# Output gates of two branches as sets of seven quarter products inside the recurrence, with a new order for VectorE and memory loaded in halves

## The reference

```python
def first_block(x, mem, ...):
    h = rms_norm(x, norm_g[l])
    p = h @ w_in[l]
    y_a = rwkv7_mix(...) * silu(z_a)                     # the recurrence
    y_b = sliding_window_sink_attn(...) * silu(z_b)
    y_c = memory_cross_attn(p_xq, mem, mem_norm_g, ...) * silu(z_c)
    gates = sigmoid(p_gate).reshape(bsz, t, 3, 1024)
    merged = (gates[:, :, 0] * (y_a @ w_proj_a) + gates[:, :, 1] * (y_b @ w_proj_b)
              + gates[:, :, 2] * (y_c @ w_proj_c))
    x = x + merged @ w_out

def hybrid_layer(x, mem, ...):                           # the second layer
    # top-k sparse attention (8 heads) beside a 31-tap causal convolution, w_out_2,
    # cross attention to a memory of 256 rows, a feed-forward net with a 3-tap convolution
return rmsnorm(x, norm_final_g)
```

## Time and profile before

| | |
|---|---|
| median of 3 runs | 1705.4 us (1705.25 to 1709.52) |
| the profiled execution's own time | 1704.97 us |
| its span | 1703.2 us |
| TensorE busy | 1610.0 us (95%) |
| VectorE busy | 1078.9 us (63%) |
| ScalarE busy | 384.4 us (23%) |
| GpSimd busy | 130.7 us (8%) |

### The profile page before, as it was taken

One profiled execution on the slowest core, in us unless ns is written; L12 is line 12 of the kernel. 1 busy time (PEld: TensorE's weight loads), 2 busy tenths in 40 slices (PEclk: granted clock), 3 DMA queues, 4 the chain that ended last, 5 costly groups with the idle time before them and its releaser, 6 DMA issues.

```text
span 1703.2 us, 23651 instructions
## 1 busy us (share of the span) xinstructions
PE 1610.0 (95%) x9170; PEld 1115.1 (65%) x9170; DVE 1078.9 (63%) x2127; ACT 384.4 (23%) x750; POOL 130.7 (8%) x121
## 2 busy tenths in 40 slices
PE   7989997899999999999999988999999999999997
PEld 6866543345555555675854456648785888888885
DVE  5976856852333333377848999566767787877453
ACT  3334344431111111131125433320301000000000
POOL 0020300031000000000007700000000000000000
PEclk9999998999999999999999998999999999999998
DMA  7212110111111111123212221122022222223331
GB/s 269 72 60 74 50 62 27 48 50 38 38 39 38 40 37 49 59 75 124 99 62 75 75 75 63 50 87 84 29 75 74 75 99 77 97 82 97 91 89 63
DMA packets 46271, 122.05 MB, mean 72 GB/s; under 512 B 5137, under 2 KB 19217, under 8 KB 45777
## 3 DMA queue, kind: packets, MB, share of 16 engines
q1 hardware_dynamic: 45072, 115.89, 20.0%
q10 hardware_dynamic: 864, 3.35, 0.5%
q0 software_dynamic: 224, 1.31, 0.2%
HBM read 118.43 MB, written 2.10 MB: 71 GB/s over the span
## 4 chain that ended last, share of the span: by engine, by line
PE 72%; DVE 23%; ACT 2%; issue 2%; DMA 1%; ACTq 0%; DVEq 0%
PE bank L608 17%; DVE arena L1796 5%; DVE arena L1787 4%; PE vpair L1264 4%; PE opair L1264 4%; PE bank L1264 3%; PE abank L1264 3%; PE opair L638 2%; PE vpair L638 2%; PE abank L1018 2%; PE vpair L1018 2%; PE opair L1293 2%; PE vpair L1293 2%; DVE tmp L1787 2%; PE abank L638 2%; DVE arena L2419 2%
## 5 line engine op out<-in xcount | busy, mean ns | idle before, releaser
L608 PE MATMUL bank<-h,ring 128*128 128x512 f32 x816 | 380.2, 606 | 1.1 <-ACTq L1401 1.1
L608 PEld LDWEIGHTS bank<-h,ring 128*128 128x128 f32 x816 | 149.0, 191 | 160.6 <-issue 152.9
L1787 DVE TENSOR_TENSOR arena<-arena,vpair 128x256 f32<-128x256 f32 x87 | 36.7, 421 | 190.3 <-PE vpair L1018 117.6
L608 PE MATMUL bank<-arena,ring 128*128 128x512 f32 (+1 forms) x320 | 122.2, 523 | 2.5 <-DVE arena L1787 2.3
L1787 DVE TENSOR_TENSOR arena<-ring 128x512 f32<-128x512 f32 (+2 forms) x132 | 78.4, 594 | 70.6 <-DMA ring<-weights 50.9
L1796 DVE SCALAR_TENSOR_TENSOR arena<-arena,cols 128x512 f32<-128x512 f32 (+1 forms) x133 | 98.2, 738 | 4.7
L608 PEld LDWEIGHTS bank<-arena,ring 128*128 128x128 f32 x320 | 59.3, 194 | 48.0 <-issue 40.2
L857 PE MATMUL vpair<-arena 128*128 128x256 f32 (+4 forms) x224 | 49.2, 451 | 29.0 <-DVE arena L1787 12.9
L1787 DVE TENSOR_TENSOR arena<-arena 128x256 f32<-128x256 f32 (+1 forms) x114 | 57.3, 503 | 6.0 <-PE bank L911 2.2
L857 PEld LDWEIGHTS vpair<-arena 64*128 64x128 f32 (+1 forms) x224 | 31.3, 207 | 45.0 <-DVE arena L1787 15.3
L2692 POOL TENSOR_TENSOR arena<-arena 128x512 f32<-128x512 f32 x43 | 55.9, 1299 | 16.6 <-ACT arena L1660 13.4
(11 more groups left out here) (359 smaller groups left out, 2985.3 us busy)
## 6 DMA issues: line engine op xcount, KB each, us to landing
ring<-weights SPq DMA_DIRECT2D x185, 512.0 KB, 3.6
ring<-weights SPq DMA_DIRECT2D x68, 128.0 KB, 2.3
x<-xt SPq DMA_DIRECT2D x8, 512.0 KB, 7.1
ring<-weights SPq DMA_DIRECT2D x40, 64.0 KB, 2.0
out<-h SPq DMA_DIRECT2D x8, 256.0 KB, 2.0
cst<-cst_in ACTq DMA_DIRECT2D x1, 1504.0 KB, 8.0
arena<-memt ACTq DMA_DIRECT2D x1, 1024.0 KB, 7.9
arena<-mem2t POOLq DMA_DIRECT2D x1, 1024.0 KB, 5.0
```

The source lines that it names most:

```text
L608: last = mm(o[:, 0:n], weight(), src, start=c == 0, stop=c == len(srcs) - 1)
L1787: do(V.tensor_tensor(out, a, b, op), sig)
```

## The change

1. **Gates of branches b and c by sets.** For each pair of tiles, one set of seven quarter products in four groups (2, 2, 2 and 1 quarters) goes through the two filling banks (`gate_set`), then two projections. An iteration has 7 + 2 + 2 = 11 quanta; the last fill is 2 and no longer 3. VectorE puts the quarters together in `gate_out` (`first_quarter` to `last_quarter`, 8 operations of 128x256 a set), ScalarE applies one tanh to both tiles, and `gated` multiplies. The four weight sums of the next set stand in `gated(n, 1)`, at the head of the next iteration; those of set 0 ahead of the loop, after a wait for `silu_done`. The weights' order in `source` follows, in more and smaller transfers.
2. **The memory in halves.** `mem[:, 0:4]` comes by ScalarE's queue as before, `mem[:, 4:8]` by SP's, ahead of all else there. Their readers wait for each half.
3. **VectorE's order at the front.** `apply_norm` stands ahead of the weight sums of set 0; the sums of sets 4 and 5 stand right behind takes 2 and 3, ahead of refinements.
4. **Paired scores.** VectorE takes the maxima of a pair of attention jobs in the first one's step (window and sparse attention).
5. **Gates of branch a.** TensorE no longer waits for `c_read` there; VectorE forms the weight sums earlier, and the squares of the second memory and the angles change places with takes.
6. **Constants.** Seven unused 128-column blocks are gone, so the transfer of 1504 KB is 1056 KB.

The diff, cut to its core:

```diff
--- before.py
+++ after.py
...
-for _name, _n in (("ones", P), ("head_ones", P), ("ident", P), ("ident64", HD), ("rot", P), ("dup0", P), ("dup1", P),
-                  ("rotdup0", P), ("rotdup1", P), ("rot2", P), ("rot2dup0", P), ("rot2dup1", P),
...
-        gt = [tmp[:, 3], thz[:, 1]]
...
+        gate_sums, gate_out = take(4, T), take(2, T)
...
+        QUARTERS = (("dve", 0), ("dve", 0), ("dve", 0), ("dve", 2 * KD))
+        stage("gates", *[*QUARTERS, V4, V4] * len(GATES))
+        GATE_SETS = len(GATES)
+        GATE_PAIRS = 7 + 2 + 2
...
-        GATED = stage_groups("gates", "gates a")
+        GATED = [("dve", 4), ("dve", 4), ("dve", 4), ("act", 2), ("dve", 4), ("dve", 4)] * GATE_SETS
...
-        source += [*range(YA, LWA), *range(V_ + 4 * KD, GLU)]
+        source += range(YA, LWA)
+        GATE0 = V_ + 4 * KD
+        for q in range(GATE0, GATE0 + 24 * len(GATES), 48):
+            for a, n in ((0, 8), (8, 4), (12, 8), (20, 4)):
+                source += [*range(q + a, q + a + n), *range(q + 24 + a, q + 24 + a + n)]
+        source += range(GATE0 + 24 * len(GATES), GLU)
...
-        GATE_PAIRS = 12
...
-                    if n or name == "gates a":
+                    if n and name == "front sets":
                         pe.wait_ge(c_read.sem, s)
                     product(d[:, 0:HT], summed(3), lambda k: h[:, 4 + k, HT:T])
...
+            def gate_set(n):
+
+                s = set_number("gates", n)
+                w = [weight() for _ in range(2 * KD)]
+                sums = set_sums("gates", n)
+
+                def product(o, lhs, rhs):
+                    for k in range(4):
+                        last = mm(o, lhs(k), rhs(k), start=k == 0, stop=k == 3)
+                    return last
+
+                def summed(i):
+                    pe.wait_ge(wsum_ready.sem, 4 * s + i + 1)
+                    return lambda k: sums[i][:, tok(k)]
+
+                o = dense_bank()
+                product(o[:, 0:HT], lambda k: w[k], lambda k: h[:, k, 0:HT])
+                yield
+                end_group(product(o[:, HT:T], lambda k: w[4 + k], lambda k: h[:, 4 + k, 0:HT]))
+                yield
+                o = dense_bank()
+                product(o[:, HT:T], summed(0), lambda k: t_h[0][:, k])
+                yield
+                end_group(product(o[:, 0:HT], summed(1), lambda k: t_h[1][:, k]))
+                yield
+                o = dense_bank()
+                product(o[:, 0:HT], summed(2), lambda k: t_h[2][:, k])
+                yield
+                end_group(product(o[:, HT:T], lambda k: w[12 + k], lambda k: t_h[3][:, k]))
+                yield
+                o = dense_bank()
+                end_group(product(o[:, 0:HT], summed(3), lambda k: h[:, 4 + k, HT:T]))
+                yield
+
+            def gate_stream(ybs, ycs):
+
+                for n in range(GATE_SETS):
+                    yield from gate_set(n)
+                    for _ in range(2):
+                        yield from dense_pairs((ybs, ycs)[n % 2])
...
-            work = stream([hs, ybs, hs, ycs] * len(GATES))
+            work = gate_stream(ybs, ycs)
...
-                    fill(work, 3)
+                    fill(work, 2)
...
             def gate():
 
-                o = dense_in()
                 n = st["gate"]
                 st["gate"] += 1
-                if n >= 2:
-                    act.wait_ge(gate_used.sem, n - 1)
-                do(fn(gt[n % 2], o[:, :], ACT.Tanh, scale=0.5), dense_act)
+                act.wait_ge(gate_summed.sem, n + 1)
+                do(fn(gate_out, gate_out, ACT.Tanh, scale=0.5), gate_th)
...
-            act.dma_start(mem, memt).then_inc(mem_in.sem, 16)
+            act.dma_start(mem[:, 0:4], memt[:, 0:4]).then_inc(mem_in.sem, 16)
...
+                act.wait_ge((mem_in if i < 4 else mem_late_in).sem, 16)
...
+                    for j in scored_in(i, n, first):
+                        scored(j)
...
-            dve.wait_ge(mem_in.sem, 16)
             for i in range(KD):
+                dve.wait_ge((mem_in if i < 4 else mem_late_in).sem, 16)
...
-                g = start[name] + n
-                if n >= 2:
+                g = start[name] + n * (6 if name == "gates" else 1)
+                if n >= 2 and name != "gates":
...
-            fast_weights("front sets", 0)
             for i in range(4):
                 dve.wait_ge(x_in[i].sem, 16)
             apply_norm("norm_g")
+            fast_weights("front sets", 0)
...
+            fast_weights("front sets", 3)
             for n in range(2):
-                fast_weights("front sets", 3 + n)
                 plain_take("front sets", 2 + n, yc[:, 2 * n:2 * n + 2, :])
+                fast_weights("front sets", 4 + n)
                 for i in range(2 * n, 2 * n + 2):
                     ri = rinv_refined(i)
                     stt(xq[:, i, :], xq[:, i, :], col("xq_g"), ri, MUL, MUL, norm_applied)
-            fast_weights("front sets", 5)
...
+            def first_quarter():
+
+                a, b = halves_of(dense_in())
+                copy(c21, a)
+                tt(c11, c21, b, ADD, dense_dve)
+
+            def second_quarter():
+
+                a, b = halves_of(dense_in())
+                tt(c21, c21, a, ADD)
+                tt(c12, c21, b, ADD, dense_dve)
+
+            def third_quarter():
+
+                a, b = halves_of(dense_in())
+                tt(c22, c12, a, ADD)
+                tt(c21, c21, a, ADD)
+                tt(c21, c21, b, ADD, dense_dve)
+
+            def last_quarter():
+
+                a, _ = halves_of(dense_in())
+                tt(c12, c12, a, ADD, dense_dve)
+                signal_now(gate_summed)
+
+            def gated(n, i):
+
+                if i and n + 1 < GATE_SETS:
+                    fast_weights("gates", n + 1)
+                dve.wait_ge(gate_th.sem, n + 1)
+                j = GATES[n // 2 * 2 + i]
+                o = dense_in()
+                stt(tmp[:, 2] if n % 2 else partial[j], gate_out[:, i, :], 1.0, o[:, :], ADD, MUL, dense_dve)
+                if n % 2:
+                    tt(partial[j], partial[j], tmp[:, 2], ADD)
+
+            reading = {"done": 0, "todo": [f for n in range(GATE_SETS) for f in (
+                first_quarter, second_quarter, third_quarter, last_quarter,
+                lambda n=n: gated(n, 0), lambda n=n: gated(n, 1))]}
+            dve.wait_ge(silu_done.sem, 12)
+            fast_weights("gates", 0)
...
+                if i == 2:
+                    fast_weights("gates a", 2)
                 ri = rinv_in(i)
                 stt(tmp[:, 0], rwy[:, i, :], col("lnx_g", i), ri, MUL, MUL)
                 stt(tmp[:, 0], tmp[:, 0], col("lnx_b", i), bonus[:, i, :], ADD, ADD)
                 tt(ya[:, i, :], tmp[:, 0], ya[:, i, :], MUL, norm_applied)
             bufs["lo"] = sq
-            fast_weights("gates a", 2)
             plain_take("gates a", 1, gates_a[:, 2:4, :])
+            fast_weights("gates a", 3)
+            angles(pos2_in, "freq2", trig_ready, 1, pos2_raw, ang)
+            plain_take("gates a", 2, gates_a[:, 4:6, :])
             for i in range(KD):
                 add_square(i, of=mem2_squares)
-            fast_weights("gates a", 3)
-            plain_take("gates a", 2, gates_a[:, 4:6, :])
-            angles(pos2_in, "freq2", trig_ready, 1, pos2_raw, ang)
...
+            sp.dma_start(mem[:, 4:8], memt[:, 4:8]).then_inc(mem_late_in.sem, 16)
```

93 lines of the change are left out of this document (36 added, 57 removed).

## The result

| | before | changed |
|---|---|---|
| median | 1707.22 us (1705.25 to 1709.52, 4 runs) | 1691.7 us (1690.65 to 1692.35, 4 runs) |
| span of the profiled execution | 1703.2 us | 1690.4 us |
| ratio | | 0.9914, interval 0.99 to 0.9929 |

Faster by 15.5 us in these runs. The four runs of before stand in two pairs, near 1705.3 and near 1709.3, so its median of 1707.22 lies between them. In three later sets of runs before had medians of 1705.2 to 1705.3, and in one of them the changed kernel 1690.25 (ratio 0.991, 0.9897 to 0.9924); the gain is 13.5 to 15.5 us, by the runs that are compared. The forecast was 1683.9, against 1704.97: 21 us were forecast, some 15 came.

A forecast was written before the change was run, and what follows sets the result against it. TensorE, nearly without gaps, was taken to bound the recurrence and VectorE the sparse attention. From 1704.97 us, -12.5 (recurrence), -1.9 (memory), -2.9 (`apply_norm`) and -3.8 (front sums) gave 1683.9 us, range 1673 to 1696.

The forecast's parts named there:

- one quantum less in eight iterations: Recurrence: each of eight iterations has 11 quanta for 12, some 1.7 us each, so 13.6 us go.
- weight sums of set 0 ahead of the first masks: First iteration of the recurrence: VectorE's sums after silu delay level 1, +1.1 us (bounds 0 and +3).
- VectorE's quarters in the levels, quarter-width quanta: Recurrence levels: 3.7 us of new operations a set hidden in VectorE's idle time, quanta of both kinds cost the same: 0.
- weight sums at the head of the iterations: Head of each iteration: four sums, 2.9 us, fit in slack of 1.5 to 1.8 us, larger with transposes: cost 0.
- memory in halves: Start: memory split over two queues, second product group near 16.7 for 18.55, -1.9 us (bounds 0 and -3.2).
- `apply_norm` first: Front set 0: put ahead of the weight sums, both TensorE waits go, -2.9 us (bounds 0 and -2.9).
- sums of sets 4 and 5: Front sets: four sums move into VectorE's idle time, its chain ends earlier, -3.8 us (bounds -1.0 and -3.8).
- Rival (b): Start: memory halves bring nothing, since bytes set the start; 1685.8 us, chance 0.13.
- Rival (a): Sparse attention: paired scores pay too, TensorE's seven waits (12.2 us) close; 1671.7 us, chance 0.12.
- (c): Front: its time is given back in a later wait, only the recurrence counts; 1692.5 us, chance 0.17.
- (d): Recurrence: the removed quantum was cover for a VectorE chain, a wait replaces it; 1697.5 us, chance 0.09.
- (e): Head of each iteration becomes the bound, slower; 1736.7 us if sums and quarters lie wholly bare, chance 0.04.

The follow-up runs named there:

- 5: The kernel before, every second gate tile of branches b and c made from six of its eight blocks, 11 full-width quanta an iteration: 1691.52 us, ratio 0.9923.
- 6: The changed kernel with the weight sums of set 0 behind the first iteration's masks instead of ahead: 1691.3 us, ratio 0.9918.
- 1: The kernel before with only the gates of branches b and c by sets and the smaller constants: 1696.41 us, ratio 0.9945.
- 9: The changed kernel with four more 128x512 sums on VectorE ahead of each of the seven in-loop sets of weight sums: 1698.95 us, ratio 0.9961.
- 3: The kernel before with the memory in halves alone: 1706.66 us, ratio 1.0001.
- 4: The changed kernel with the memory loaded whole on ScalarE's queue as before: 1691.3 us, ratio 0.9916.
- 2: The changed kernel without the gates by sets and without the smaller constants: 1701.46 us, ratio 0.998.
- 7: The changed kernel with both halves of the memory on SP's queue, ahead of the weights: 1691.57 us, ratio 0.9918.
- 11: The changed kernel with the weight sums of set 0 behind the first iteration's masks, run again: 1691.57 us, ratio 0.9915.
- 12: The changed kernel run once more, unaltered, in one call with the masks-first repeat: 1690.25 us, ratio 0.991.

## Why the prediction was right, and by how much its terms were off

| term | forecast | measured | from |
|---|---|---|---|
| one quantum less in eight iterations | -13.6 | -13.7 | 5 |
| weight sums of set 0 ahead of the first masks | +1.1 | +1.0 | 6 |
| VectorE's quarters in the levels, quarter-width quanta | 0 | +2.1 (+2.4 less the fifth iteration's wait) | 1, 5, 6 |
| weight sums at the head of the iterations | 0 | 0, cover 1.55 to 1.95 | 9 |
| memory in halves | -1.9 | 0 | 3, 4 |
| `apply_norm` first | -2.9 | -2.55 | 2 |
| sums of sets 4 and 5 | -3.8 | -3.8 | 2 |
| paired scores, gates of branch a | 0 | 0 | 2, table |

The measured time lies 7.8 us above the forecast, well inside the range, and the three largest terms (the gates, `apply_norm`, the sums of sets 4 and 5) came where they were forecast. With all of it the measured parts make -10.6 - 2.55 - 3.8 = -17.0 us, and the medians -13.5 to -15.5. The rest is in single product groups that run slower behind a wait in some profiles. One of them is in the last stretch, from the end of the sparse attention to the end: the same sixteen records took 8.83 us for 7.13 in nine of the thirteen new profiles, behind a wait of 2.0 us in all of them. The first row is before, the second changed:

```profile
1116.80 7.13 PE L1221 MATMUL vpair<-arena,ring 128*128 128x512 f32 x16 [1.99 <-DVE arena L1796]
```
```profile
1102.90 8.83 PE L1259 MATMUL vpair<-arena,ring 128*128 128x512 f32 x16 [2.00 <-DVE arena L1832]
```

Of the changed kernel and its variants (experiments 4, 6, 7, 9, 11 and 12) six profiles in seven have it, of the others three in seven. Whether the change makes it more frequent, or chance does, no run shows.

Two steps failed. The first is the sentence that the quarters in the levels "are hidden". They are shorter than VectorE's idle time there, which is what I looked at, but the next level's sum starts 0.07 us late behind them, at three places in an iteration. With the quarter-width quanta a little longer (1.99 for 1.98, or 1.93 for 1.91 to the next group), where the prediction had "quanta of both kinds cost the same", that makes 0.3 us an iteration. A count of idle time cannot show that; it needs the time from the product to the sum.

The second is the memory. I took the second group (18.55) as waiting for panels. It had no wait in its row: TensorE ran from 9.57 to 26 without a gap, so the start alone set it, and the start hung on the half on ScalarE's queue, which landed near 8.7 for 9.1. Rival (b) was right that this term is 0. The section "Issuing engines are not separate DMA queues" of the Trainium skill's page "DMA: Bandwidth & Descriptors" says that transfers run on the same 16 DMA engines and interleave, whichever engine issued them; the bytes moved from 2 to 9 us agree (2.61 before, 2.36 changed and 2.42 MB in experiment 7). The term was not 0 for want of an earlier start, though: in experiment 7 TensorE did start 0.8 us earlier and lost it to the third panel.

Two smaller errors cost little. The prediction had the slack at the head larger where transposes stand ahead of level 1, and experiment 9 found it smaller, 1.55 for 1.95 us. And it took both of TensorE's waits for `h` (2.9 us) as gained, where one of 0.58 for a weight sum came in and 2.55 us were left.

Rival (a) can be judged in the sparse attention. Seven waits of 12.2 us on the scores are gone, and in their place TensorE waits in more and shorter pieces:

```profile
PE abank L929 <- DVE arena L1829: 9.8, 8, 2.5
PE opair L910 <- DVE arena L1835: 8.2, 7, 1.7
```

That is 18 us where it was 12.2 and 1.5. The clock is 1.00 for 0.92, TensorE is busy for 4.4 us less, and the stretch isn't shorter. VectorE is busy for 84.12 of the 90 us, as before for 84.09. That fits VectorE being the bound, whose work an order doesn't shorten; it is argued, for no run takes work off VectorE there. The gates of branch a look the same: the wait of 2.52 us is gone, but a new one of 2.10 stands ahead of the projection's first group, and that on VectorE behind it is 2.76 for 2.31:

```profile
751.09 3.67 PE L605 MATMUL bank<-arena,ring 128*128 128x512 f32 x8 [2.10 <-issue]
757.52 3.70 PE L605 MATMUL bank<-arena,ring 128*128 128x512 f32 x8 [2.76 <-DVE arena L1823]
```

The waits moved and their sum is 4.86 us for 4.83. From the first of these gates to the wait of 1.39 us in w_out, which both kernels have, it is 93.3 us for 93.5. Rivals (c), (d) and (e) fall with experiments 2, 5 and 9.

## What to carry to other kernels

Removing work from an engine that has no gaps paid here as forecast (13.7 us for 13.6), and it can be priced alone beforehand by leaving that work out (experiment 5). What it adds elsewhere is not free just because it fits into idle time; look at the latency from one engine's product to the other's next operation, with and without other work between. And before a gain is credited to an earlier transfer, look whether the later group has a wait at all: without one, only the start of the gapless run counts.

## What the runs showed of the hardware

TensorE's products at the start run at about half speed (records of 794 ns for 379) for a time that differs from run to run. The same 32 products took 8.59 to 10.23 us in fourteen profiles, whatever the kernel; in the changed kernel single ones took 379 to 794 ns:

```profile
L949 PE MATMUL bank<-arena,ring x64: 379/379/794, 9.2 to 26.4; 128*128 128x256 f32 x64
```

(minimum, median, maximum in ns.) The granted clock reads 1.00 in that stretch, so that column doesn't show it. In the recurrence the column does: in the seventh iteration of the changed kernel it is 0.96 after waits of 1.05 and 0.60 us, with the same two waits and 1.00 in the repeat. And the stretch behind the wait of 4.62 us ahead of the ones-product has a granted clock of 0.50, the lower of its two levels, 1.2 GHz:

```profile
120.00:124.00 4.00, 3.86 (x5) 1.81 (x6) 0.25 (x1) 2.01 (x4) 0.00 (x0) 0.50 0.00 0
```

Why it falls after the short waits in one execution and not in the other stays open. Such a fall makes its group 1.5 to 1.7 us longer, more than several of the parts that were under study, but it costs that only where no wait on another engine follows soon: in experiment 1 the group behind the 2.52 us took 5.35 us for 3.72, and the next wait shrank from 2.31 to 0.68 us; in experiment 6 one took 5.37 for 3.67, and the next wait shrank from 2.76 to 1.07. Two falls that do cost, in branch a's projection and in the last stretch, both stand in the profile of experiment 3 (1707.99 us, of the upper group of its runs) and neither in that of before (1704.97). The two groups of runs some 3 to 4 us apart may be executions with and without them; of each of these two kernels one execution was profiled, so that is not shown.
